# Where a transformer block's output weights are scaled and split: among the grouped-query attention steps, or during the key and value tiles

## The reference

```python
mod_l = (silu_c @ w_mod[l] + b_mod[l])[:, None, :]
sh1, sc1, gt1, sh2, sc2, gt2 = jnp.split(mod_l, 6, axis=-1)
pl = modulate(rms_norm(xl, g_mix[l]), sh1, sc1) @ w_in[l]
...
gqa_l = gqa_latent(q_l, [k_c, k_l], [v_c, v_l])
na_l = natten_latent(nq_l, nk_l, nv_l, nk_c, nv_c, na_rpb[l])
hyo_l = hyena_mixer(hy_l, filt_l, hy_conv_w[l], hy_conv_b[l], hy_skip[l])
mix_l = jnp.concatenate([hyo_l, gqa_l, na_l], axis=-1) @ w_out[l]
xl = xl + gt1 * mix_l
xl = xl + gt2 * swiglu(modulate(rms_norm(xl, g_ffn[l]), sh2, sc2), w_ffn_in[l], w_ffn_out[l])
```

## Time and profile before

| | |
|---|---|
| median of three runs | 1267.82 us (1267.33 to 1268.02) |
| the profiled execution | 1269.27 us |
| its span in the profile | 1267.5 us |
| granted TensorE clock, mean over the span | 0.999 |
| instructions | 22616 |
| bytes moved | 158.89 MB |
| read from and written to device memory | 135.95 MB, 19.93 MB |

### The profile page before, as it was taken

How to read it: one execution, slowest core, us unless ns; L and a number is a source line. 1 busy time by engine, 2 the same in 40 slices (tenths; PEclk the granted TensorE clock), 3 DMA queues, 4 the chain that set the end, 5 groups by cost and what they waited for, 6 DMA issues and landing times. The chain is left out here.

```text
span 1267.5 us, 22616 instructions
## 1 busy us (share of the span) xinstructions
PE 1242.6 (98%) x7808; PEld 655.8 (52%) x7808; DVE 905.6 (71%) x1510; ACT 648.1 (51%) x1236; POOL 345.2 (27%) x341
## 2 busy tenths in 40 slices
PE   8999999999999999999999999999999999999997
PEld 1564656556675666664454444444444444444443
DVE  3879886766778999964458866666666675566587
ACT  2532224557779999973135654444454543312424
POOL 0100000114678899850003222333332220000001
PEclk9999999999999999999999999999999999999999
DMA  9628812335210120121130332222223305997963
GB/s 360 266 83 316 288 45 87 113 84 151 68 35 1 35 104 29 33 85 50 50 89 12 92 92 75 81 67 67 76 89 91 91 18 156 332 331 264 344 231 133
DMA packets 108164, 158.89 MB, mean 125 GB/s; under 512 B 8384, under 2 KB 67264, under 8 KB 106816
## 3 DMA queue, kind: packets, MB, share of 16 engines
q1 hardware_dynamic: 108096, 158.00, 36.8%
HBM read 135.95 MB, written 19.93 MB: 123 GB/s over the span
## 5 line engine op out<-in xcount | busy, mean ns | idle before, releaser
L1206 PE MATMUL PS<-arena 128*128 128x512 f16 (+9 forms) x7208 | 1201.1, 327 | 16.0 <-DMA arena<-in_w_mod 5.5
L1206 PEld LDWEIGHTS PS<-arena 128*128 128x128 f16 (+3 forms) x7208 | 604.7, 102 | 586.5 <-issue 39.5
L2894 DVE SCALAR_TENSOR_TENSOR arena<-arena 128x512 f16<-128x512 f32 x148 | 120.9, 823 | 76.6 <-ACT arena L2182 76.6
L2182 ACT ACTIVATE arena<-arena 128x512 f16<-128x512 f32 x140 | 87.6, 629 | 130.4 <-PE PS L1206 130.4
L2786 DVE TENSOR_REDUCE arena<-PS 128x1 f32<-128x512 f32 (+1 forms) x160 | 106.4, 680 | 9.1 <-PE PS L1206 9.1
L2294 ACT ACTIVATE arena<-arena 128x512 f16<-128x512 f32 x77 | 48.2, 629 | 123.3 <-DVE arena L3045 74.2
L2094 ACT ACTIVATE arena<-PS 128x512 f16<-128x512 f32 x140 | 88.3, 631 | 1.2 <-PE PS L1206 0.7
L1173 POOL TENSOR_TENSOR arena<-arena 128x512 f32<-128x512 f32 x20 | 26.6, 1334 | 222.2 <-DMA arena<-in_w_ffn_in 194.0
L1077 POOL TENSOR_TENSOR arena<-arena 128x512 f16<-128x512 f32 x64 | 74.1, 1159 | 9.4 <-ACT arena L2097 8.1
L1200 POOL TENSOR_TENSOR arena<-arena 128x1 f32<-128x1 f32 x8 | 4.7, 598 | 236.0 <-DVE arena L3186 236.0
L2810 DVE TENSOR_TENSOR arena<-PS,arena 128x512 f16<-128x512 f32 x96 | 65.4, 681 | 4.0 <-ACT PS L2097 3.9
(11 more groups left out here) (204 smaller groups left out, 1156.8 us busy)
## 6 DMA issues: line engine op xcount, KB each, us to landing
arena<-in_w_ffn_out SPq DMA_DIRECT2D x121, 256.0 KB, 5.1
arena<-in_w_mod SPq DMA_DIRECT2D x23, 1024.0 KB, 7.4
arena<-in_w_ffn_in SPq DMA_DIRECT2D x88, 256.0 KB, 3.0
arena<-in_w_in SPq DMA_DIRECT2D x9, 1024.0 KB, 5.5
left_operands<-arena SPq DMA_DIRECT2D x33, 256.0 KB, 2.2
arena<-left_operands SPq DMA_DIRECT2D x3, 2816.0 KB, 11.7
arena<-lay_bias SPq DMA_DIRECT2D x12, 512.0 KB, 4.0
arena<-in_x SPq DMA_DIRECT2D x2, 2048.0 KB, 13.9
```

What stands on the lines that cost most here:

```text
L1206: return pe.matmul(out, lhsT, rhs, start=start, stop=stop, skip_group_check=True)
L2182: act.activation(aS[n % RING][:, 0], weight_block(p, b), ACT.Copy, scale=WS).then_inc(blk_hi, 1)
L2894: dve.scalar_tensor_tensor(dst[:, 1], src, WS, dst[:, 0], ALU.mult, ALU.subtract).then_inc(blk_lo, 1)
```

## The change

The work on `w_out` is moved from the GQA groups to the key and value tiles, in eight halves of 128 x 1024 (512 KB each), and the result is kept in DRAM:
- SP: two of the halves are loaded right behind the issue of the fourth query-key-value chunk, behind a new wait for `y_rdy` 4 (their buffers, `wo_raw` and `wo_parts`, lie where hyena's last arrays were). The loads of the four late chunks 33 to 36, and of query chunks 37 and 38, stand behind these in the queue. `keep_wo(h)` waits for half h, issues the load of half h+2 and the store of half h; the eight calls stand among the near-value and bias loads. When the last neighbourhood output is made, four loads of 1 MB bring the split weights back (`woS`).
- GpSimd: `wo_scale(h)` at unit 11+h and `wo_low(h)` at unit 12+h, behind `inverse_roots` of that unit and ahead of the next scale. `scale_out`, `out_hi` and `out_lo` are gone.
- ScalarE: `wo_high(h)`, a cast of 128 x 1024, at unit 12+h, right behind `from_psum` (the eighth in the first neighbourhood unit).
- VectorE: the late rows' sum changes its buffer after four rows; one wait is added.
- TensorE: only the wait ahead of `project_out` is another one.

```diff
@@ -46,14 +46,13 @@
 CHUNKS = (["mod"] * 8 + ["ff", "ff", "hy", "hy", "late", "late", "hy"] + ["late"] * 6 + ["qkv", "qkv"] + ["late"] * 4
-          + ["fwd", "fwd", "inv", "inv"] + ["qkv"] * 2 + ["late"] * 4 + ["qkv"] * 2 + ["wo"] * 4)
-N_EARLY = len(CHUNKS) - 4
+          + ["fwd", "fwd", "inv", "inv"] + ["qkv"] * 2 + ["late"] * 4 + ["qkv"] * 2)
...
 def chunk_slot(c):
-    return c % 4 if c < N_EARLY else (c - N_EARLY) % 2
+    return c % 4
...
@@ -427,7 +427,8 @@
         mrow = f32(Z, 2, GW)
-        macc = [f32(o, GW) for o in (Z, Z + 4, Z, Z + 8)]
+        macc = [f32(o, GW) for o in (Z, Z + 4, Z, 104)]
+        macc_begun = f32(Z + 20, GW)
...
@@ -473,6 +474,8 @@
+        wo_raw = [f32(Z + 8 + 4 * i, 2, 512) for i in range(2)]
+        wo_parts = [f16(Z + 16 + 4 * i, 2, 2, 512) for i in range(2)]
...
@@ -559,6 +562,8 @@
         pr_tc = sem("qk_transposed_copied")
+        wo_raw_in, wo_out, wo_in = (cols_in, small_in), (x_in[0], rest_in), gn_in
+        wo_scaled, wo_hi = mlp_arg, mlp_h
...
@@ -804,11 +814,20 @@
                         sp.wait_ge(late_used, 2 * n_of_kind(before, "late"))
-                    elif kind == "wo":
-                        sp.wait_ge(wo_split, n_of_kind(before, "wo"))
...
+
+            def load_wo(h):
+                k, n = 4 * (h // 4) + 2 * (h % 2), h // 2 % 2
+                sp.dma_start(wo_raw[h % 2], w_out[:, k:k + 2, 512 * n:512 * n + 512]).then_inc(wo_raw_in[h % 2], 16)
+
+            def keep_wo(h):
+                sp.wait_ge(wo_split, h + 1)
+                if h + 2 < N_WO:
+                    load_wo(h + 2)
+                sp.dma_start(wo_kept[:, h // 2, :, 2 * (h % 2):2 * (h % 2) + 2], wo_parts[h % 2])\
+                    .then_inc(wo_out[h % 2], 16)
...
@@ -843,6 +862,10 @@
                     load(c, w_in[:, kh:kh + 4, col:col + 512], (4, 512))
+                if c == chunk_index("qkv", 3):
+                    sp.wait_ge(y_rdy, 4)
+                    for h in range(2):
+                        load_wo(h)
...
@@ -865,33 +888,37 @@
+            for h in range(4):
+                keep_wo(h)
...
                 load_bias(n)
+            keep_wo(4)
...
                 load_near(cw)
+            keep_wo(5)
+            keep_wo(6)
...
                 load_bias(n)
+            keep_wo(7)
...
                              allow_slow_non_contiguous=True).then_inc(gates_out, 16)
-            sp.wait_ge(s_max, n_scored(BiasPiece(BIAS_EARLY - 1).units_done - 1))
-            for n in range(2):
-                load(chunk_index("wo", n), w_out[:, 0:4, 512 * n:512 * n + 512], (4, 512))
...
                 load_bias(n)
-            for n in range(2, 4):
-                load(chunk_index("wo", n), w_out[:, 4:8, 512 * (n % 2):512 * (n % 2) + 512], (4, 512))
...
             sp.wait_ge(o_mm, NNA)
+            sp.wait_ge(pr_r, n_normed(NU - 1))
+            for n in range(4):
+                sp.dma_start(woS[n], wo_kept[:, n]).then_inc(wo_in, 16)
...
@@ -1037,26 +1063,15 @@
-            def scale_out(i):
-
-                n, k = i // 4, i % 4
-                c = chunk_index("wo", n)
-                r = raw(c, 4, 512)[:, k]
-                if k == 0:
-                    arrived(pool, c)
-                own.step(pool.tensor_scalar(r, r, WS / HS if n < 2 and k < 2 else WS, None, ALU.mult))
-
-            def out_hi(i):
-                own.wait()
-                own.step(pool.tensor_copy(woS[i // 4][:, 0, i % 4], raw(chunk_index("wo", i // 4), 4, 512)[:, i % 4]))
-
-            def out_lo(i):
-                n, k = i // 4, i % 4
-                own.wait()
-                ins = pool.tensor_tensor(woS[n][:, 1, k], raw(chunk_index("wo", n), 4, 512)[:, k], woS[n][:, 0, k],
-                                         ALU.subtract)
-                if k == 3:
-                    ins.then_inc(wo_split, 1)
+            def wo_scale(h):
+                pool.wait_ge(wo_raw_in[h % 2], 16 + 16 * (h // 2) + 16)
+                r = flat(wo_raw[h % 2])
+                pool.tensor_scalar(r, r, WS / HS if h in (0, 2) else WS, None, ALU.mult).then_inc(wo_scaled, 1)
+
+            def wo_low(h):
+                pool.wait_ge(wo_hi, 3 + h + 1)
+                pool.tensor_tensor(flat(wo_parts[h % 2][:, 1]), flat(wo_raw[h % 2]), flat(wo_parts[h % 2][:, 0]),
+                                   ALU.subtract).then_inc(wo_split, 1)
...
@@ -1122,6 +1137,11 @@
                 inverse_roots(u)
+                h = u - GROUP0[1] - 1
+                if h >= 1:
+                    wo_low(h - 1)
+                if 0 <= h < N_WO:
+                    wo_scale(h)
...
@@ -1133,22 +1153,9 @@
                     high_queries(0)
-                for i in ((), (0,), (1,), (2,), (3,), (4, 5), (6, 7), ())[u - GROUP0[0]]:
-                    scale_out(i)
-
-            pool.wait_ge(s_mm, n_scored(NNA - 1))
...
             for g in range(NGROUP):
-                i = g + (g > 2)
-                if 4 <= g < 12:
-                    scale_out(g + 4)
                 for n, k in enumerate(POOL_TILES):
-                    if n == 1 and i < 16:
-                        out_hi(i)
-                    if n == 3 and i < 16:
-                        out_lo(i)
-                    if n == 3 and g == 2:
-                        out_hi(3)
-                        out_lo(3)
...
@@ -2005,6 +2012,9 @@
                 if g == 0:
+                    if t == 0:
+                        for h in range(N_WO - 2, N_WO):
+                            wo_stored(act, h)
...
@@ -2045,8 +2055,18 @@
                     output_hi(2 * u - 11)
+            def wo_high(h):
+                act.wait_ge(wo_scaled, 3 + h + 1)
+                if h == 1:
+                    act.wait_ge(late_used, 24 + LATE_MOVE + 1)
+                elif h >= 2:
+                    wo_stored(act, h - 2)
+                act.copy(flat(wo_parts[h % 2][:, 0]), flat(wo_raw[h % 2])).then_inc(wo_hi, 1)
...
                 from_psum(u)
+                if u >= GROUP0[1] + 2:
+                    wo_high(u - GROUP0[1] - 2)
...
@@ -2116,6 +2136,7 @@
             from_psum(first - 1)
+            wo_high(N_WO - 1)
...
@@ -2507,13 +2528,18 @@
                 acc, s = macc[g], silu_c[:, 2 * kp + i, 0:1]
+                old = acc
+                if g == 3:
+                    acc, old = [macc_begun if m < LATE_MOVE else macc[3] for m in (2 * kp + i, 2 * kp + i - 1)]
+                    if 2 * kp + i == LATE_MOVE:
+                        dve.wait_ge(pr_mm, GROUP0[1] + NC)
...
                     dve.wait_ge(late_used, 2 * n + i)
-                    ins = dve.scalar_tensor_tensor(acc, w[:, i], s, acc, ALU.mult, ALU.add)
+                    ins = dve.scalar_tensor_tensor(acc, w[:, i], s, old, ALU.mult, ALU.add)
...
                 ins.then_inc(late_used, 1)
```

More of the change, by code:

```diff
@@ L74, in n_split @@
 def n_split(c):
-    return sum(k not in AS_IS and k != "wo" for k in CHUNKS[:c + 1])
+    return sum(k not in AS_IS for k in CHUNKS[:c + 1])
 STEPS = [(p, b) for p in ("P2", "P1", "P5", "P6", "P7", "P3", "P4") for b in range(2)]
@@ L354, in build @@
         t2_kept = nc.dram_tensor("weight_sum_rows", (P, KQ, 512), F32, kind="Internal").ap()
+        wo_kept = nc.dram_tensor("split_output_weights", (P, 4, 2, 4, 512), F16, kind="Internal").ap()
         left_kept = nc.dram_tensor("left_operands", (3, P, KQ * 1024), F16, kind="Internal").ap()
@@ L734, in mix_parts, with wo_stored @@
             return ps, [mixT[:, part, 4 + n % 2, half] for part in range(2)]
+        N_WO, LATE_MOVE = 8, 4
+        def wo_stored(eng, h):
+            eng.wait_ge(wo_out[h % 2], (16, N_REST)[h % 2] + 16 * (h // 2) + 16)
         def arrived(eng, c, more=0):
@@ L818, in _ @@
             n_of["mod"] = 1
-            for c in range(1, N_EARLY):
+            for c in range(1, len(CHUNKS)):
                 if c == 1:
@@ L904, in _ @@
             for b in range(2):
-                sp.wait_ge(wo_split, 3 + b)
                 for a in ("A11", "A12", "A21", "A22"):
@@ L1730, in project_out @@
                         between[k]()
-            pe.wait_ge(wo_split, 4)
+            pe.wait_ge(wo_in, 32 + 64)
             pe.wait_ge(y_rdy, 4)
```

## The result

The changed kernel takes 1286.12 us (median of four runs, 1285.52 to 1287.06), the one before 1267.62 us beside it: the ratio is 1.0146, with an interval of 1.0129 to 1.0164. That is 18.5 us slower. Forecast were 1290.8 us and +23.0. The profiled execution took 1286.23 us.

What follows compares the result with a forecast made beforehand. TensorE, busy 98%, was taken as the bound, so its waits counted. 4.8 + 19.6 - 1.4 = +23.0 took the profiled 1269.27 to 1292.3 us, median 1290.8; own range 1284 to 1297, with rivals 1273 to 1298.

Steps and rivals of the forecast that it cites:

- Step 1: Key and value tiles: late chunks issued behind hyena's wait and two `w_out` halves delay VectorE's late row, then TensorE: +4.8 us.
- The train's second MB: First late chunk, queued behind two 0.5 MB halves of `w_out`, taken to land 7.4 us after hyena's output.
- Step 2: Key and value tiles: GpSimd's new scales and low halves and VectorE's two-SBUF-input operations exclude each other: +19.6 us.
- the circle: Units 14 to 16: GpSimd's and VectorE's mutually excluding operations from one power to the next, 8.9 us against 5.62.
- rival A: Tiles: only two-input operations exclude each other, so the scale runs beside VectorE; 8.0 us there, total 1279.2 us, chance 0.12.
- the mark of being wrong: Prediction wrong if TensorE idles under 15 or over 30 us before 320 us, or GQA's length changes by over 4.
- Rival E: TensorE's clock halves after waits of 3 to 5 us: 1293.4 us in small form, over 1298 with chance 0.05.
- Step 3: Key and value tiles: ScalarE's eight casts, 1.0 to 1.1 us each, fit its idle time: 0 us.
- Step 4: GQA groups: GpSimd relieved of the work, TensorE's waits of 0.96 and 0.43 us go: -1.4 us.
- Step 5: Transfers: 4 MB of added stores and 4 MB of loads, with the reload well ahead of `project_out`: 0 us.
- widths of 4.7 to 5.3: Bounds in us for GpSimd's scale and low half of 128x1024 per unit together, taken as 5.0.

Runs made afterwards that it cites:

- E2: Kernel before, with only the wait for hyena's output put ahead of the four late chunks, no load of `w_out` there: 1271.61 us, ratio 1.0030.
- E1: Changed kernel with the wait for hyena's output and first two output-weight loads moved behind the four late chunks: 1276.68 us, ratio to before 1.0068.
- E5: E1 with GpSimd's two-input low half replaced by a one-input product with 1.0 of the same size: 1280.02 us, ratio to before 1.0096.
- E6: E1 with GpSimd's one-input scale replaced by a two-input sum of the buffer with itself: 1283.07 us, ratio to before 1.0111.
- E4: E1 with GpSimd's scale 2 columns wide instead of 1024, the low half kept whole: 1271.70 us, ratio to before 1.0025.
- E8: E1 with the split made by ScalarE (scaled high half) and VectorE (low half), GpSimd taking no part: 1276.50 us, ratio to before 1.0061.
- E10: E8 with one store and one load of the output weights issued ahead of the first near-value and bias loads: 1284.00 us, ratio to before 1.0114.
- E3: E1 with GpSimd's low half 2 columns wide and a second ScalarE cast in its place, scale kept whole: 1273.13 us, ratio to before 1.0043.
- E11: Kernel before with one high and one low half in each of 16 GQA groups, none double, measured a second time: 1267.51 us, ratio 0.9989.

## Why the prediction was right, and where it was off

The direction was right, and both causes named were real: late chunks, and GpSimd's work holding VectorE. That the total came within 5 us was in part luck: the tiles were priced 11.6 us too high, and 4.2 us of late landing and low clock that the sum did not have made up for part of it.

**Step 1, the late chunks: right in its mechanism, low in its size.** The row waited, and behind it the low parts and the transposes, in the order given. The term was 4.8; measured are 6.1. The train's second MB was set at 7.4 us after hyena's output and came at 8.6 (E2 splits it: 5.1 for the wait and first landing, 3.5 for the halves in front). The measured 6.1 lies under the term's upper bound of 6.6. E1 shows it by removing it.

**Step 2, the exclusion: right for the low half, wrong for two thirds of the scale.** The step that failed is the scale's 2.86 us in the circle 0.70 + 2.16 + 2.86 + 0.34 + 1.2 + 1.14 + 0.5 = 8.9. It holds VectorE 0.9 us, not for its length. With 0.9 in its place the circle is 6.9; 7.02 was measured. The low half's 2.16 (2.13 measured), the late row's and `lo_half`'s terms stand. So 16.0 us for units 12 to 16 became 5.6 and the whole stage 19.6 became some 8: 5.6 and 2.4. That the two-input kind counts is shown by E5 and E6, the scale's part of the circle by E4 (6.1 without it, 0.9 less).

The prediction's own signs for this step did not come. The late rows took 1.27 us and not 2 to 4, TensorE's waits were 0.26 to 1.22 us and not 2 to 4, and "only the low half stretches them" was its sign for rival A. From 225 to 320 us TensorE idles 95 - 82.73 = 12.3 us (1.4 before), under the 15 that it named as the mark of being wrong. Only with the 6.4 us from ahead of 200 us, which the change has no part in, is it 18.7, between its 15 and 30:

```profile
0.00:200.00 200.00, 193.56 (x891) 103.22 (x892) 153.47 (x213) 65.03 (x96) 4.31 (x11) 0.99 0.58 215
225.00:320.00 95.00, 82.73 (x556) 46.51 (x554) 68.44 (x146) 53.54 (x122) 51.70 (x35) 0.95 0.64 205
```

The rule of the Trainium skill, "SBUF — State Buffer", section "Who interferes with whom", which gives the scale its full length too, is right here for two-input operations on both sides (3.44 us in E6) and not for the one-input product: its hold ends after 0.9 us of 2.8. The same section says that a two-input VectorE operation contends with what GpSimd reads and not with what it only writes. A product that has read all its input after 0.9 us, and only writes from then on, would look like this; no run here shows its inside, so that stays a reading.

**Rival A** was right that the late row and `lo_half` run beside the scale, but gave nothing for its first 0.9 us. Of the tiles it had the better picture than the forecast. Its price for the tiles (8.0) is the measured one, in part by chance: its circle was 7.4 for the measured 7.02 (the forecast's 8.9), and E4 gained 5 us where A allowed 2. Its total, 1279.2, is 7 us under the measured, since it had neither the 1.3 us more of step 1 nor the clock.

**Rival E, the clock, happened in its small form**: 1.3 us after the 6 us wait, granted 0.86 over 225 to 250 us, and 1.6 more at 293 us. The price for the first stop, 2.6 us, was twice what it cost. The prediction had counted against this rival that TensorE, busy 0.77 us of the first 5, showed a clock of 1.00. That reading was wrong. The trace before has the first five matmuls, and five of the same form after 12 us:

```profile
4.23 4.37 PE L1206 MATMUL PS<-arena 128*2 128x512 f32 x5 [4.23 <-DMA arena<-in_w_mod]
```
```profile
12.17 2.31 PE L1206 MATMUL PS<-arena 128*2 128x512 f32 x5 [1.28 <-DMA arena<-in_w_mod]
```

The first take 4.37 us for 2.31, whatever the clock row says: a start at nearly half rate, in the very rows that were read against one. The Trainium skill, "TensorE: Matmul & The Clock Gate", section "What's actually happening", has an idle engine at 1.2 GHz. The trace agrees for the 6.0 us stop, with a granted clock of 0.50, that is 1.2 GHz, from 238.4 to 245.0 us. It does not explain the fall at 293 us, where TensorE's last wait was of 1.16 us.

**Step 3, 0: right.** The casts take 1.05 us each (1.0 to 1.1 forecast), and none of TensorE's waits from 225 to 330 us ended with one. **Step 4, -1.4: right**, -1.1 measured; GQA's pace is ScalarE's, 24.90 of 25. **Step 5, 0: right** as to the reload, on which TensorE never waited. But GpSimd's last scale waited 1.57 us for its half of `w_out` to land (at 297.24), at the head of the neighbourhood units; what part of the 2.4 us lost there that is, is open. E8 and E10 show how near the stores stand to the path.

**The sum.** 4.8 + 19.6 - 1.4 = 23.0 was forecast. Measured are 6.1 + 1.3 for the first stop, 5.6 + 2.4 for the tiles and what follows, 1.6 for the second low clock, -1.1 in GQA: 15.9, and 0.8 from before the change's first effect. The bounds named for the forecast, 1284 to 1297, do not follow from the terms: with the train's 2.5 to 6.6 and widths of 4.7 to 5.3 in six units the same sum gives about 1286.6 to 1294.3, an estimate.

## What to carry to other kernels

An idle engine is not free room: ask which of its operations can run beside the neighbour's, by kind of operand, not by length. A load that "has time" may stand in a queue ahead of one that has none, so a wait put into a queue costs what is behind it. And a stop of TensorE can be paid twice: the 6.0 us here cost 1.3 us more in clock. From what length on is not shown. After E2's stop of 2.45 us the granted clock stayed at 1.00 (236 to 245 us), around E8's of 2.39 it was 0.66 (288 to 293 us).

## What was not expected of the hardware

- GpSimd's one-input product of 128x1024 float32 (2.8 us) held VectorE's two-input operations for 0.9 us from its start. Beside the two pairs of low parts above: in E3 286.29 began 0.49 in and lost 0.4; 270.83 in E5 began 0.5 in and lost 0.85, the hold having begun late, behind the late row. Later in it, VectorE's 1.27 and 1.21 us operations lost nothing.
- VectorE's tiny one-input product L2667 (0.17 us) behaves the other way. In E1 it began 2.07 us into a scale and lasted to the scale's end, 0.77 us:

```profile
282.59 0.77 DVE L2667 TENSOR_SCALAR arena<-arena 128x2 f32<-128x2 f32 x1
```
```profile
280.52 2.82 POOL L1069 TENSOR_SCALAR arena<-arena 128x1024 f32<-128x1024 f32 x1
```

- The late row that writes to another buffer than it reads took 2.05 us for 1.27 in the changed kernel (256.39), 0.1 us behind the start of a scale. It is the same hold and not the buffer: in E5 that row (247.90), 1.11 us into a product, took 1.27, and a row on one buffer (263.15), 0.16 us behind the start of one, took 2.06.
- A stretch of half clock at 136 us, worth up to 1.5 us, shows in some profiled executions (the changed kernel, E2, E4, E5) and not in others (before, E1, E3, E6, E8 to E11; there was no E7), with no edit in that place. It is most of the 0.8 us from before 230 us. What sets it off is open.
